# Turning the inverse row sums of attention with one transpose a round, from a tile that the vector engine fills

## The reference

```
def blocked_attention(q, k, v, scale):          # latent attention, grouped attention
    s = jnp.einsum('bqkgd,bskd->bkgqs', q_i, k).astype(jnp.float32) * scale
    p = jax.nn.softmax(s, axis=-1).astype(v.dtype)
    return jnp.einsum('bkgqs,bskd->bqkgd', p, v)

def neighbourhood_attention(...):               # the same with a bias from a table
def dsa_sparse_attention(...):                  # the same with a mask of chosen keys
```

## Time and profile before

| what | us |
|---|---|
| median of 3 runs | 2246.71 |
| lowest and highest of them | 2243.39, 2250.3 |
| span of the profiled execution, first to last instruction | 2246.0 |
| PE busy in the span | 2163.1 (96%) |
| DVE busy | 1082.7 (48%) |
| ACT busy | 462.0 (21%) |
| POOL busy | 139.0 (6%) |

### The profile page before, as it was taken

How to read it: one execution, slowest core, us unless ns; L and a number is a source line. 1 busy time by engine, 2 the same in 40 slices (tenths; PEclk the granted TensorE clock), 3 DMA queues, 4 the chain that set the end, 5 groups by cost and what they waited for, 6 DMA issues and landing times.

```text
span 2246.0 us, 33411 instructions
## 1 busy us (share of the span) xinstructions
PE 2163.1 (96%) x14268; PEld 1514.0 (67%) x14268; DVE 1082.7 (48%) x1944; ACT 462.0 (21%) x1004; POOL 139.0 (6%) x148
## 2 busy tenths in 40 slices
PE   6999999989999999999998999999999999999998
PEld 3447878554688885456466885686785488768646
DVE  2675555477645446652353114585324428642443
ACT  2433211352300000031253000223210022311001
POOL 0004333000000000011100000002000000200000
PEclk9999999999999999999999999999999999999999
DMA  8221444504322224445103444333344433234441
GB/s 325 75 75 40 153 153 155 177 20 187 150 75 94 93 76 150 170 144 136 57 8 131 158 154 169 141 113 113 131 150 169 155 145 119 107 131 150 169 170 74
DMA packets 41665, 289.86 MB, mean 129 GB/s; under 512 B 5040, under 2 KB 6448, under 8 KB 7216
## 3 DMA queue, kind: packets, MB, share of 16 engines
q1 hardware_dynamic: 39344, 279.99, 34.0%
q0 software_dynamic: 1312, 3.15, 1.1%
q10 hardware_dynamic: 864, 4.61, 0.5%
HBM read 286.15 MB, written 1.05 MB: 128 GB/s over the span
## 4 chain that ended last, share of the span: by engine, by line
PE 91%; DVE 5%; ACT 2%; issue 1%; DMA 1%; SPq 0%; ACTq 0%; DVEq 0%
PE banks L1009 22%; PE banks L414 15%; PE banks L1571 12%; PE banks L1470 7%; PE banks L2726 6%; PE banks L2068 6%; PE banks L1751 2%; PE banks L1775 2%; PE banks L649 1%; PE banks L789 1%; PE banks L1771 1%; PE banks L2720 1%; PE banks L452 1%; PE banks L502 1%; PE banks L804 1%
## 5 line engine op out<-in xcount | busy, mean ns | idle before, releaser
L414 PE MATMUL banks<-normed,weight_ring 128*128 128x256 f32 (+1 forms) x1280 | 294.8, 393 | 7.8 <-DVE normed L566 5.7
L414 PEld LDWEIGHTS banks<-normed,weight_ring 128*128 128x128 f32 x1280 | 245.2, 192 | 56.7 <-issue 15.3
L1009 PE MATMUL banks<-arena 128*128 128x512 f32 x392 | 186.2, 593 | 0.7 <-DVE arena L1627 0.5
L1470 PE MATMUL banks<-normed,weight_ring 128*128 128x256 f32 x704 | 153.9, 382 | 3.4 <-ACT normed L580 3.4
L1009 PE MATMUL banks<-weight_ring,arena 128*128 128x512 f32 x338 | 157.1, 593 | 0.0
L1470 PEld LDWEIGHTS banks<-normed,weight_ring 128*128 128x128 f32 x704 | 134.9, 192 | 22.4 <-ACT normed L580 3.8
L1009 PEld LDWEIGHTS banks<-arena 128*128 128x128 f32 x392 | 74.1, 190 | 93.6 <-issue 92.3
L2726 PE MATMUL banks<-normed,weight_ring 128*128 128x256 f32 x576 | 127.6, 381 | 5.8 <-DVE normed L566 2.9
L2068 PE MATMUL banks<-normed,weight_ring 128*128 128x512 f32 x288 | 126.1, 593 | 0.0
L2726 PEld LDWEIGHTS banks<-normed,weight_ring 128*128 128x128 f32 x576 | 108.6, 190 | 22.6 <-issue 5.0
L974 DVE TENSOR_TENSOR arena<-weight_ring 128x512 f32<-128x512 f32 x67 | 46.2, 690 | 144.2 <-PE banks L1009 144.2
(11 more groups left out here) (455 smaller groups left out, 3422.4 us busy)
## 6 DMA issues: line engine op xcount, KB each, us to landing
weight_ring<-in_weights SPq DMA_DIRECT2D x266, 1024.0 KB, 4.8
residual<-in_tokens ACTq DMA_DIRECT2D x1, 2048.0 KB, 12.7
mix<-in_rpb POOLq DMA_DIRECT2D x32, 64.0 KB, 3.7
constants<-in_const ACTq DMA_DIRECT2D x1, 1953.5 KB, 12.6
out<-residual SPq DMA_DIRECT2D x1, 1024.0 KB, 4.8
branch<-arena POOLq DMA_DIRECT2D x1, 512.0 KB, 4.8
normed<-in_ple POOLq DMA_DIRECT2D x1, 512.0 KB, 3.7
vector_params<-in_vectors ACTq DMA_DIRECT2D x1, 223.0 KB, 5.8
```

What stands on the lines that cost most here:

```text
L414: mm = pe.matmul(K.psum[lo:hi, banks[m % nb], 0:T], K.block(first[m] + k)[:, lo:hi], rhs(k), start=(k == 0), stop=(k == n_k - 1))
L1009: return pe.matmul(self.bank[i], left, b, start=(p == 0), stop=(p == n - 1))
L1470: mm = pe.matmul(K.bank(i % 4, T), K.block(first[i] + k), u[:, k, 0:T], start=(k == 0), stop=(k == KT - 1))
```

## The change

DVE, after the reciprocals of a round, waits for them and copies them into a new tile of 128 by 128: 64 columns hold the reciprocal of head 0, 64 that of head 1. There are two such tiles, used in turn. PE transposes the tile with one transpose in place of the two products. The wait for the earlier turning (`spread_inverses`) now stands before the copy and not before the reciprocal. A new semaphore, `wide_inverses`, tells PE of the copy. The new tiles are 256 columns of `attention_buffers`; in the odd mixer the tile `tmp`, taken after them, no longer fits in its first region and goes to the second.

```
--- before.py
+++ after.py
@@ -753,14 +753,14 @@
-    names = {"scores": n, "maxima": n, "probabilities": n, "turned": n, "row_inverses": len(rounds), "spread_inverses": len(rounds),
-             "weighed": len(rounds), "inverses_kept": len(outs), "group_out": len(outs)}
+    names = {"scores": n, "maxima": n, "probabilities": n, "turned": n, "row_inverses": len(rounds), "wide_inverses": len(rounds),
+             "spread_inverses": len(rounds), "weighed": len(rounds), "inverses_kept": len(outs), "group_out": len(outs)}
...
-    prob, probT, small, spread = buf
+    prob, probT, small, spread, wide = buf
@@ -805,13 +805,10 @@
         def spread_inverse(r):
-            pe.wait_ge(sg["row_inverses"].sem, at["row_inverses"] + r + 1)
+            pe.wait_ge(sg["wide_inverses"].sem, at["wide_inverses"] + r + 1)
             if r % 4 == 0 and r:
                 pe.wait_ge(sg["inverses_kept"].sem, at["inverses_kept"] + r // 4)
-            for j in range(2):
-                s = 2 * r % 4 + j
-                mm = pe.matmul(K.psum[64 * j:64 * j + 64, 7, r % 4 * P:r % 4 * P + P], inverse[:, s:s + 1].to_broadcast([P, 64]), K.c("ident"), start=True, stop=True)
-            mm.then_inc(sg["spread_inverses"].sem, 1)
+            pe.transpose(K.bank(7)[:, r % 4 * P:r % 4 * P + P], wide[:, r % 2, :], K.c("ident")).then_inc(sg["spread_inverses"].sem, 1)
@@ -866,10 +863,12 @@
                 dve.wait_ge(sg["probabilities"].sem, at["probabilities"] + 2 * r + 2)
+                s = 2 * r % 4
+                dve.reciprocal(inverse[:, s:s + 2], total[:, s:s + 2]).then_inc(sg["row_inverses"].sem, 1)
+                dve.wait_ge(sg["row_inverses"].sem, at["row_inverses"] + r + 1)
                 if r >= 2:
                     dve.wait_ge(sg["spread_inverses"].sem, at["spread_inverses"] + r - 1)
-                s = 2 * r % 4
-                dve.reciprocal(inverse[:, s:s + 2], total[:, s:s + 2]).then_inc(sg["row_inverses"].sem, 1)
+                dve.tensor_copy(wide[:, r % 2, :].rearrange("p (j n) -> p j n", j=2), bc(inverse[:, s:s + 2], 2, 64)).then_inc(sg["wide_inverses"].sem, 1)
                 if beside:
                     beside(dve, r)
@@ -2489,7 +2488,7 @@
 def attention_buffers(K, area):
-    return area.get(4, 512), area.get(4, 4, P), K.small, area.get(512)
+    return area.get(4, 512), area.get(4, 4, P), K.small, area.get(512), area.get(2, P)
```

## The result

The changed kernel takes 2258.66 us, the median of 20 runs (2248.69 to 2266.0); the kernel before, measured beside it in 20 runs, takes 2249.02. The ratio is 1.0044, with a 95% interval of 1.0032 to 1.0055: slower by 0.44%, 9.6 us. The forecast was 2245.2 us, between 2240 and 2251, with no measurable change. It was wrong.

What follows compares the result with a forecast made beforehand. PE was taken to bound the kernel, except DVE's ring in the even stage's first eight rounds. PE -4.0, copy +2.05 and late tile +0.4 made -1.5 us on 2246.71: 2245.2 us, range 2240 to 2251.

Steps and rivals of the forecast that it cites:

- The saving on PE: Grouped-attention rounds on the chain: one transpose for two identity products saves 0.11 us a round, 4.0 us in all.
- the start-up of 0.15: PE's cost where the weights' shape changes; forecast to move from the identity products to the weighing, not be saved.
- 36 rounds: Rounds with the products on the chain: 7 even, 15 odd, 7 in each sparse stage; 0.11 us saved in each.
- The copy on DVE: New copy after the reciprocals, 0.226 us plus 0.03 start; adds 2.05 us over the even stage's first eight rounds.
- the ring: Even stage's first eight rounds: reciprocals, DVE's three operations, first maximum, ACT, next reciprocals; 4.34 us, to grow by 0.256.
- the 0.26 falls before maxima that PE's scores hold up anyway: Even stage from round 8 on: the copy's added DVE time was claimed to cost nothing.
- The late tile: PE waits for reciprocal plus copy: 0.2 us in round 0 of each sparse stage, 0.4 in all, nothing elsewhere.
- The mechanism that makes it larger: Rival: copies wait for POOL's operations in odd and sparse stages; 2247.9 us, or 2251.8 at full waits; chance 0.32.
- The clock: Sign of error: the granted clock, 1.00 or nearly so in all these stages, falls; no size or chance given.
- The saved start-up: Rival: PE's 0.15 us is saved, not moved to the weighing; 0.26 a round, 2239.7 us; chance 0.08.
- the absorbing ring: Rival: slack in the even stage's first eight rounds hides the copy's 2.05 us; 2243.1 us; chance 0.10.

Runs made afterwards that it cites:

- the reduction: The changed kernel with its copy written as a maximum over an axis of one element; 2255.12 us, ratio 1.0033 to the kernel before.
- g3: The kernel before with the change in the sparse stages alone, its copy written as a maximum over one element; 2246.49 us, ratio 1.0006.
- f3: The kernel before with seven more small DVE products, some 1.4 us, at the end of the even mixer; 2249.95 us, ratio 1.0008.
- h1: The kernel before with the change in the odd stage alone; 2252.41 us, ratio 1.0023.
- h3: All stages changed, copy as a maximum, DVE's three operations moved, six repeated products in the odd feed-forward; 2246.07 us, ratio 0.9988 to the kernel before.
- h4: The kernel before with ten repeated 128x256 products in the odd feed-forward, 4.3 us of PE work; 2255.32 us, ratio 1.0028.
- e1: The kernel before run again without an edit, as a control; 2249.50 us, ratio 1.0008.
- g2: The change in all stages, copy as a maximum over one element, DVE's three operations moved behind the next maxima; 2243.79 us, ratio 0.9993 to the kernel before.

## Why the prediction was wrong

**The saving on PE** held in its mechanism. A round saves 0.11 us, the transpose is 0.109, and the start-up of 0.15 moved to the weighing. What failed is the count of 36 rounds: the stage saves that only where nothing else becomes late. By the stages: in the odd one 0.5 instead of 15 x 0.11 = 1.65 (1.35 with the reduction); in a sparse one 0.06 with the reduction, since the last round saves nothing (its weighing takes 1.16 us in g3, 0.90 before) and the first two tiles come late.

**The copy on DVE.** The size, 0.226 us, and the ring, 0.26 a round, were right: the eight reciprocals of the ring rounds and the next lie 36.71 us apart (455.01 to 491.72), 2.2 more than before, with 2.05 forecast. Wrong was "the 0.26 falls before maxima that PE's scores hold up anyway" for the other eight. In those rounds where the multiplication of L880 stands in the same place, the copy comes on top of it:

```profile
503.12 0.23 DVE L871 COPY arena<-attention_small 128x128 f32<-128x128 f32 x1
503.26 0.68 DVE L880 TENSOR_TENSOR mix<-banks,arena 128x512 f32<-128x512 f32 x1
503.86 0.74 DVE L860 TENSOR_REDUCE attention_small<-banks 128x1 f32<-128x256 f32 x2
504.52 0.41 DVE L776 COPY arena<-banks 128x256 f32<-128x256 f32 x1
```

The next reciprocal is at 505.63, 2.71 us after the one at 502.92; before, it was 2.47 (503.39 to 505.86). From the ninth reciprocal to the last the kernel before takes 15.88 us and the changed one 16.03: where 0.8 was to be saved, 0.15 is lost. The even stage costs 2.4 in place of the forecast's 1.3 (2.05 less seven times 0.11).

**The late tile** is the first step that failed. It was put at 0.4 us, all of it in the sparse stages, and at nothing in the odd stage, where the first two copies were held too (0.99 and 1.13 us) and the transpose (L811) waited 0.6 us for them; the reduction takes 0.9 us off that stage. The mechanism that makes it larger stood among the rivals with 0.32, priced at +0.78 for a sparse stage (1.55 less seven times 0.11). It is what happened, with +1.05; without the held copies (g3) the stage is at -0.06. The argument against it, that "the copy has one input, and no row of that kind stands beside POOL", was only the lack of a row. Absence of a row is no evidence, and the Trainium skill's page spoke for the rival. By stages, measured against forecast: even +2.4 for +1.3, odd -0.5 for -1.65, each sparse one +1.05 for -0.57. The sum is +4.0 us in place of -1.5, about 2251, the very end of the range.

**The clock** is the second, and larger, step that failed: the sum had no term for it. "I am wrong ... if the granted clock ... falls" was said, without a chance or a price. Of the 9.6 us, 4.0 are work by the stages, and some 6 are left, which go with a mean clock lower by 0.0056. That division is not sharp. By the runs' slope this clock would be worth about 10 us alone; but not every low stretch costs (the even stage of f3 took 56.96 us with one of 3.4 us at its start, and that of the kernel before 56.96 with none), so the slope is an upper bound and 4 + 10 is not to be added up. That the change brings the lower clock is shown by its 20 and 12 runs beside the 152 of the kernel before, and h1 shows it in work that was not touched. That it comes from where work lies in time rests on h3, and weakly on h4, and is not proven. Which part of the change moves it most was not settled: each part alone (even, odd, sparse) costs 2.8, 5.1 and 4.8 us, together 12.7, more than the whole, each with an interval of some 3 us to either side.

**The saved start-up** and **the absorbing ring** are excluded by the 1.02 of L822 and the ring's 4.60.

What to have instead: keep the two products and move DVE's three other operations (f4), 0.19% below the kernel before, with an interval that ends at 0.9996. That is a small gain: the control e1 alone lay 0.08% off.

## What to carry to other kernels

Read who else uses on-chip memory before putting a copy on DVE: beside POOL a copy of 0.226 us can take 1.25, and the same work written as a reduction keeps its 0.286. A copy that is cheap in most rounds is paid in those where DVE already has an extra operation, so lay out DVE's queue for each kind of round, not for the average one. In a kernel that is PE-bound nearly throughout, where the granted clock dips at times, a change of one or two microseconds is not judged by one trace: compare the mean clock over the runs, and try the same shift with useless work first. Read the price of such useless work from its own trace, too: here it was twice what was planned, and that took away the force of one experiment.

## What was not expected of the hardware

- Work that was not touched got another clock: an unchanged sparse stage took 22.84 us instead of 19.94 in the kernel whose odd stage is 0.5 us shorter, and 2.6 us of added products took away all of another kernel's runs at 0.985.
- The low clock was granted in PE's busiest stretches too. The windows of h1 before and in the low stretch of its first sparse stage:

```profile
1524.30:1531.10 6.80, 5.35 (x45) 4.64 (x44) 2.39 (x7) 3.03 (x6) 1.42 (x2) 1.00 0.43 141
1531.10:1537.90 6.80, 6.80 (x36) 5.00 (x35) 1.97 (x9) 2.81 (x15) 6.41 (x7) 0.50 0.49 205
```

At 1.00 PE was busy with matmuls for 5.35 of 6.80 us, and with its weight loads counted too it stood still for 0.11; then it was granted 0.50, and worked without a pause. The kernel before has the same stretch, with the same busy times and the same 0.11 us of standing still, and 1.00 behind it:

```profile
1525.70:1532.50 6.80, 5.35 (x45) 4.64 (x44) 2.39 (x7) 3.03 (x6) 1.42 (x2) 1.00 0.44 146
1532.50:1539.30 6.80, 6.80 (x57) 4.96 (x56) 2.66 (x13) 3.94 (x21) 6.41 (x7) 1.00 0.48 201
```

So what PE did in the 6.8 us before does not tell the two cases apart.
- One kernel can have two times some 10 us apart by its clock (g2: 0.990 to 0.994 and 0.984 to 0.985), where one of its traces alone would show the worse: its profiled execution has a span of 2248.3 us at 0.985.
